# Other column orders for the moving operand and the bank in the last layer's up products

## The reference

```
def conv_ffn(xn, w_up, conv_w, conv_b, w_down):
    s_len = xn.shape[1]
    hdn = xn @ w_up
    hp = jnp.pad(hdn, ((0, 0), (CONV_W - 1, 0), (0, 0)))
    acc = conv_b
    for j in range(CONV_W):
        acc = acc + conv_w[j] * hp[:, j:j + s_len]
    g, u = jnp.split(acc, 2, axis=-1)
    return (jax.nn.gelu(g, approximate=False) * u) @ w_down
```

## Time and profile before

| | |
|---|---|
| Device time, median of 2 runs | 3561.99 us (3561.03 to 3562.94) |
| Span of the profiled execution | 3557.1 us |
| Median less the span | 4.9 us |
| PE busy | 3502.0 us, 98% of the span |
| PE weight loads busy | 2932.2 us, 82% |
| VectorE busy | 2226.9 us, 63% |
| ScalarE busy | 1679.6 us, 47% |
| DMA | 101 GB/s on average |

### The profile page before, as it was taken

How to read it: one execution, slowest core, us unless ns; L and a number is a source line. 1 busy time by engine, 2 the same in 40 slices (tenths; PEclk the granted TensorE clock), 3 DMA queues, 4 the chain that set the end, 5 groups by cost and what they waited for, 6 DMA issues and landing times.

```text
span 3557.1 us, 49763 instructions
## 1 busy us (share of the span) xinstructions
PE 3502.0 (98%) x19256; PEld 2932.2 (82%) x19256; DVE 2226.9 (63%) x4229; ACT 1679.6 (47%) x3243; POOL 111.3 (3%) x132
## 2 busy tenths in 40 slices
PE   9999999999999999999999999999999999999999
PEld 7898878877888987998888877888977677788887
DVE  5566656556775667566665566765676786666643
ACT  5354455554353545454555543553455443444432
POOL 0010000000000100010000000001000000000000
PEclk9999999999999999999999999999999999999999
DMA  5474331112335743574221112255522222233332
GB/s 154 131 175 143 116 95 48 45 47 72 90 105 138 173 122 98 140 172 125 83 66 47 47 60 91 93 134 151 152 79 86 69 66 84 77 94 93 95 95 86
DMA packets 198276, 358.86 MB, mean 101 GB/s; under 512 B 22102, under 2 KB 26359, under 8 KB 198040
## 3 DMA queue, kind: packets, MB, share of 16 engines
q1 hardware_dynamic: 178840, 321.32, 29.8%
q0 software_dynamic: 18432, 33.56, 5.6%
q10 hardware_dynamic: 768, 0.79, 0.1%
HBM read 350.60 MB, written 4.72 MB: 100 GB/s over the span
## 4 chain that ended last, share of the span: by engine, by line
PE 93%; DVE 4%; ACT 2%; issue 1%; DMA 0%; DVEq 0%; ACTq 0%
PE bank L2490 21%; PE bank L2499 21%; PE bank L2491 21%; PE bank L2525 6%; PE bank L2527 6%; PE bank L2528 6%; PE bank L2478 2%; PE bank L2473 1%; PE bank L2568 1%; PE bank L2661 1%; PE bank L2671 1%; PE bank L2536 1%; PE bank L2759 1%; PE bank L2588 1%; DVE w_lo L3235 0%
## 5 line engine op out<-in xcount | busy, mean ns | idle before, releaser
L2490 PE MATMUL bank<-page_r,w_hi 128*128 128x512 f32 (+1 forms) x3446 | 1383.4, 401 | 21.9 <-DVE w_lo L3235 14.7
L2499 PE MATMUL bank<-page_r,w_lo 128*128 128x512 f32 (+1 forms) x3446 | 1359.7, 395 | 0.0
L2491 PE MATMUL bank<-page_r,w_hi 128*128 128x512 f32 (+1 forms) x3446 | 1349.8, 392 | 0.0
L2490 PEld LDWEIGHTS bank<-page_r,w_hi 128*128 128x128 f32 x3446 | 650.0, 189 | 182.5 <-DVE w_lo L3235 18.8
L2813 ACT ACTIVATE w_hi<-raw 128x512 fp32r<-128x512 f32 x864 | 532.8, 626 | 558.3 <-PE bank L2499 550.1
L2499 PEld LDWEIGHTS bank<-page_r,w_lo 128*128 128x128 f32 x3446 | 649.2, 188 | 145.7
L2491 PEld LDWEIGHTS bank<-page_r,w_hi 128*128 128x128 f32 x3446 | 649.9, 189 | 141.6 <-issue 3.6
L3235 DVE TENSOR_TENSOR w_lo<-raw,w_hi 128x512 fp32r<-128x512 f32 x864 | 574.9, 686 | 150.2 <-ACT w_hi L2813 149.8
L2525 PE MATMUL bank<-page_r,w_hi 128*128 128x256 f32 x1792 | 503.7, 281 | 2.5 <-DVE w_lo L3253 2.5
L2528 PE MATMUL bank<-page_r,w_lo 128*128 128x256 f32 x1792 | 503.4, 281 | 0.0
L2527 PE MATMUL bank<-page_r,w_hi 128*128 128x256 f32 x1792 | 503.4, 281 | 0.0
(11 more groups left out here) (322 smaller groups left out, 3462.9 us busy)
## 6 DMA issues: line engine op xcount, KB each, us to landing
raw<-weights SPq DMA_DIRECT2D x864, 256.0 KB, 2.7
raw<-pairs SPq DMA_DIRECT2D x320, 256.0 KB, 3.3
raw<-pairs POOLq DMA_DIRECT2D x128, 256.0 KB, 5.8
page_f<-x_t SPq DMA_DIRECT2D x8, 256.0 KB, 5.2
bias_rows<-page_f SPq DMA_DIRECT2D x8, 256.0 KB, 2.0
page_f<-bias_rows SPq DMA_DIRECT2D x8, 256.0 KB, 3.9
out_t<-page_f SPq DMA_DIRECT2D x12, 128.0 KB, 1.8
cst<-consts SPq DMA_DIRECT2D x4, 272.0 KB, 3.5
```

Of the source, the lines that this page charges most:

```text
L2490: self.e.matmul(o, hi, X.hi[kt], start=first, stop=False)
L2491: self.e.matmul(o, hi, X.lo[kt], start=False, stop=False)
L2499: last = self.e.matmul(o, lo, X.hi[kt], start=False, stop=final)
```

## The change

In the 44 column tiles of `w_up_2`, the number of the tile modulo 5 picks a form. Form 0 (9 tiles) is as before. Forms 1 to 3 (9 tiles each) give the same three matmuls another order of columns, the same for the moving operand and for the bank, so that each column still lands at its own address. Form 4 (8 tiles) keeps the order of columns and swaps the second and third matmul of the block. The forms by columns:

- form 1, `halves_by_twos`: two columns of the first half of 256, two of the second half, the next two of the first half, and so on
- form 2, `halves_by_fours`: the same with four columns at a time
- form 3, `twos_by_parity`: columns 0, 1, 4, 5, 8, 9, ... first, then 2, 3, 6, 7, ...
- form 4: as before in columns; the matmuls go high by high, rest of the weights by high, high by rest

```diff
+def halves_by_twos(ap):
+
+    return ap.rearrange("p (a c e) -> p c a e", a=2, e=2)
+
+
+def halves_by_fours(ap):
+
+    return ap.rearrange("p (a c e) -> p c a e", a=2, e=4)
+
+
+def twos_by_parity(ap):
+
+    return ap.rearrange("p (c a e) -> p a c e", a=2, e=2)
+
+
+WALKS = (halves_by_twos, halves_by_fours, twos_by_parity, lambda ap: ap)
 
 
 def percol(s16, h):
@@ -2487,6 +2505,21 @@
         self.clear(b)
         self.wait_ge(self.m.s_lo, s + 1)
         self.wait_ge(*X.ready[kt])
+        walk = self.order[-1][1] % 5 if self.order[-1][0] == "w_up_2" and gain is None and n == SEQ else 0
+        if walk:
+            walked = WALKS[walk - 1]
+            o, x_hi, x_lo = walked(o), walked(X.hi[kt]), walked(X.lo[kt])
+            if walk == 4:
+                self.e.matmul(o, hi, x_hi, start=first, stop=False)
+                self.e.matmul(o, lo, x_hi, start=False, stop=False)
+                last = self.e.matmul(o, hi, x_lo, start=False, stop=final)
+            else:
+                self.e.matmul(o, hi, x_hi, start=first, stop=False)
+                self.e.matmul(o, hi, x_lo, start=False, stop=False)
+                last = self.e.matmul(o, lo, x_hi, start=False, stop=final)
+            if signals:
+                last.then_inc(self.m.s_gemm, 1)
+            return
         self.e.matmul(o, hi, X.hi[kt], start=first, stop=False)
```

## The result

The changed kernel takes 3634.76 us (3633.68 to 3635.83, 2 runs) against 3561.99 us, 72.8 us or 2.1% more; the ratio is 1.0209 with a 95% interval of 1.0191 to 1.0227. The forecast was no change, and the time lies above the range's 3612 us. The interval excludes no change, but it lies on both sides of 2%. The profiled execution's span grew from 3557.1 to 3631.9 us, 74.8 us.

The account below looks back on a forecast made before the run. The prediction took TensorE's streaming of its matmuls to bound the stage. Its terms, 192 x 0 for the swap and 648 x 0 for the walks, summed to 0, so 3562 us as before, range 3550 to 3612 us.

Parts of the forecast that it names:

- What bounds the kernel: In the up and down products, TensorE's matmul stream sets the time; every nanosecond added to a matmul moves the end.
- The counts: In the up products' column tiles, forms 1 to 3 have 216 matmuls each, together 648, and form 4 has 192.
- Form 4 at nothing: Swapped matmuls of form 4: a change of weights costs no more than keeping them, 192 x 0 = 0.
- Forms 1 to 3 at nothing: Walked matmuls of forms 1 to 3: the column orders do not change the pace, 648 x 0 = 0.
- the one strided row: A small 64-column product taking every other run of 8 or more columns: mean matmul 269 ns, like its plain neighbour.
- The sign that was passed over: 512-column matmuls stream at 93% of what the granted clock would allow, held by something the rows do not name.
- the second rival: Walked matmuls: only runs of two (forms 1 and 3) are slow, 85 us, 3647 us, or 3663 at double; chance 0.07.
- The first rival: All 648 walked matmuls: output or read port pays for each jump, 3690 us, or 3713 at double time; chance 0.12.
- My last sign: Walked matmuls: the prediction is wrong if a run of two is enough to lower the pace by half.
- The range: Whole kernel, 3550 to 3612 us: holds the forecast and the third rival, a partial loss, together 0.80.
- The fourth rival: Walks are joined back to plain order on the way to the chip, same 3562 us; chance inside the forecast's 0.70.
- The gain: Walked matmuls: at most 20.0 ns less each, 13 us or 0.4%; more than 2% faster had chance 0.01.

Follow-up runs that it names:

- e10: Kernel before, with every 512-column product reading and writing runs of four columns in turn from 32 equal parts: 3500.82 us, ratio 0.9831.
- e11: Kernel before, with 512-column products in runs of four from 32 parts and 256-column products in runs of four from sixteen: 3477.95 us, ratio 0.9767.
- e1: Kernel before with form 4's swap alone, the walks of forms 1 to 3 undone: 3561.05 us against 3560.84, ratio 1.0001.
- e5: Kernel before with one read pattern per column tile (shifted, repeated, two-byte columns, narrower weights): aligned runs of four 230.0 ns, two columns further 456.2, repeated columns 216.0.
- e3: Kernel before with forms 1 to 3 walking only the bank, the moving operand read in address order, form 4 undone: 3560.51 us, ratio 0.9999.
- e8: Table repeating the fast column orders in other tiles, with 256-column orders added: 226.8 ns for runs of eight from sixteen parts, plain 233.4 ns.

## Why the prediction was wrong, point by point

**What bounds the kernel**: right. All of the added time of TensorE arrived at the end (72.2 us busy, 74.8 us of span), nothing hid any of it, and a gain later (e10, e11) arrived likewise.

**The counts**: right; 216, 216, 216 and 192 are the counts by which the sum closes at 72.8 us.

**Form 4 at nothing**: right, 1.0001 in e1.

**Forms 1 to 3 at nothing**: this step failed. It is "Between these ends I take zero: the one strided row that there is shows no cost on either side". The row had runs of eight or more columns, each of which fills whole aligned groups of 16 bytes, and runs of two fill half of one. It was not the nearest row to the question but one on the other side of the point where the cost begins. I had also written that it was paced by the weight load and bounds the stream weakly, and then let it decide. The second reason, that runs stay at least two columns long and aligned to 8 bytes, was the condition of the bank, which costs nothing anyway; the read wants 16. Measured in place of 0: 21.0, 4.3 and 47.5 us.

**The sign that was passed over** is in the first part: 0.449 ns a column where the clock would allow 0.417, "by something that these rows do not name". e5 names it: the same columns repeated run at 216 ns, so plain order was already held by the read. A stream that is bound by its read has no slack for a read that uses half of what it brings. From that the second rival (only runs of two are slow, 432 x 196.7 = 85 us, chance 0.07) deserved far more than its chance. It comes nearest to what happened: forms 1 and 3 cost 68.5 of the 72.8 us. Three things in it were off. Form 2 did not keep its pace but cost 4.3 us. Its reason was that a jump after every second column is not hidden, but jumps are not the price: 128 of them cost nothing in (64,4). And it took 197 ns for both forms where they measured 97 and 220. The order of form 1 comes back to a group after one other, that of form 3 after 127; that this makes the difference is likely, but not shown. That 85 us lie near 72.8 is thus in part luck.

**The first rival** (output port or read port alike, 0.12) did not happen in its size or on the bank's side: the bank has no part (e3), and runs of four cost 20 ns. Its sign, all three forms longer, did appear, so the lengths did not tell the two rivals apart as cleanly as I had written. My last sign, a run of two that lowers the pace by half, is what form 3 showed: 453.4 against 233.4 ns. **The range** ended at one form at the slow pace, 3612 us; it had no place for two. **The fourth rival** (the walks are joined back to plain order) is excluded by the read patterns in the records. **The gain** of up to 20 ns a matmul did not come with these orders; (32,4), which I had not thought of, gained 6.4 of them.

## What to carry to other kernels

Before pricing a new access pattern, compare the distance between starts with the columns over the granted clock: if the stream is slower than that, ask which side holds it, because that side has no slack. For a moving operand of four-byte columns count the aligned groups of 16 bytes that each pass touches, some 1.8 ns each (here 1.7 to 2.2 by the order, 1.3 to 1.5 where two or three parts alternate in runs of two), and keep runs at four aligned columns or more; the bank was written in runs of two or four at no cost in the three orders tried. An order of parts has to be measured: the count does not say which are faster than plain. A strided row of the old trace is evidence only for runs that fill the same groups as the new ones.

## What the runs showed of the hardware that was not expected

- A read order can be quicker than address order: 227.0 ns in (32,4) and 226.8 in (16,8) (e8) against 233.4 for 512 four-byte columns, 114.3 against 118.3 for 256 in (16,4), worth 82 us on this kernel.
- The distance between parts matters beyond the groups: with 128 groups each, parts 16, 8, 32, 256, 128 and 64 columns apart took 227, 233, 241 to 247, 253, 267 and 279 ns. What the distance does is not explained.
- Two-byte columns in plain order run at 216.1 ns, at the array's own pace. Four-byte ones did so only where columns were repeated; with 512 different ones and 128 weight columns the best was some 226.7 ns.
